# Rows of u and v side by side: one 8 KB gather per expert slot, in a ring of eight pairs

## What is computed

```
def peer(h, w_query, sub_keys, u, v):        # u, v: (16384, 1024) per layer
    q = h @ w_query                          # 8 heads, two halves of 128
    s = q . sub_keys                         # 2 x 128 scores per head
    top_s, top_i = top_k(s, 16)              # per half
    best_s, best_pos = top_k(all 256 sums, 16)
    expert = ...                             # 16 numbers per token and head
    gate = softmax(best_s)
    act = gelu(h . u[expert])                # one dot product of 1024 per expert
    y += (gate * act) * v[expert]            # summed over 8 heads x 16 experts
```

## Time and profile before

| | |
|---|---|
| median of 3 runs | 1996.8 us (1992.76 to 1998.14) |
| profiled execution | 1994.14 us |
| its span, first to last instruction | 1992.4 us |
| mean granted TensorE clock | 0.815 |
| busy: PE, DVE, ACT, POOL | 1480.2, 1171.5, 279.1, 1025.0 us |
| DMA bytes | 669.91 MB, mean 336 GB/s |

### The profile page before, as it was taken

One profiled execution on the slowest core, in us unless ns is written; L12 is line 12 of the kernel. 1 busy time (PEld: TensorE's weight loads), 2 busy tenths in 40 slices (PEclk: granted clock), 3 DMA queues, 4 the chain that ended last, 5 costly groups with the idle time before them and its releaser, 6 DMA issues.

```text
span 1992.4 us, 18966 instructions
## 1 busy us (share of the span) xinstructions
PE 1480.2 (74%) x6422; PEld 589.7 (30%) x6422; DVE 1171.5 (59%) x2700; ACT 279.1 (14%) x539; POOL 1025.0 (51%) x1099
## 2 busy tenths in 40 slices
PE   6978999784577656767788886677797766666666
PEld 5736666464233210102223222022232210101100
DVE  3541000158777757687669636966776587776752
ACT  2141111211101101001212111012321110010000
POOL 2000000004777766677456655775566577677674
PEclk9988999877788765668996988689888975667678
DMA  9123346106999999999999999999999999999998
GB/s 332 58 80 135 130 163 256 75 22 207 383 409 409 409 409 410 396 410 409 409 406 372 410 409 393 410 409 409 404 337 409 410 409 409 406 410 408 391 404 326
DMA packets 189385, 669.91 MB, mean 336 GB/s; under 512 B 19806, under 2 KB 20960, under 8 KB 188016
## 3 DMA queue, kind: packets, MB, share of 16 engines
q0 software_dynamic: 152064, 553.72, 70.6%
q1 hardware_dynamic: 37232, 115.09, 15.2%
HBM read 667.68 MB, written 1.05 MB: 336 GB/s over the span
## 4 chain that ended last, share of the span: by engine, by line
DMA 32%; PE 15%; DVE 13%; POOL 12%; issue 6%; DVEq 2%; ACT 1%; POOLq 0%; ACTq 0%
DMA big<-in_peer_v,expert 25%; POOL big L506 12%; DVE big L569 8%; DMA big<-in_peer_u,expert 7%; PE ps L552 5%; PE ps L692 3%; PE ps L535 2%; DVEq L446 2%; PE ps L334 2%; PE ps L786 1%; PE ps L788 1%; PE ps L1658 0%; DVE residual L599 0%; PE ps L696 0%; DVE half_v L452 0%
## 5 line engine op out<-in xcount | busy, mean ns | idle before, releaser
L552 PE MATMUL ps<-big,diag 128*32 128x512 f32 (+1 forms) x2112 | 712.7, 794 | 434.5 <-DMA big<-in_peer_v,expert 399.9
L569 DVE CUSTOM_DVE_ANT_0 big<-big,ps 128x1024 f32<-128x1024 f32 x528 | 625.8, 1218 | 345.5 <-DMA big<-in_peer_u,expert 241.5
L506 POOL DMA_INDIRECT big<-in_peer_u,expert x528 | 502.1, 951 | 301.0 <-issue 131.1
L506 POOL DMA_INDIRECT big<-in_peer_v,expert x528 | 506.3, 959 | 257.2 <-PE ps L552 143.0
L552 PEld LDWEIGHTS ps<-big,diag 128*32 128x32 f32 (+1 forms) x2112 | 83.7, 120 | 968.1 <-DMA big<-in_peer_v,expert 851.6
L692 PE MATMUL ps<-big 128*128 128x512 f32 x384 | 199.0, 642 | 0.0
L1586 POOL MEMSET big<- 128x128 f32 x3 | 0.5, 203 | 374.1 <-POOLq L1450 374.1
L230 DVE RECIPROCAL stats<-stats 128x1 f32<-128x1 f32 (+1 forms) x17 | 2.7, 161 | 252.0 <-ACT stats L224 251.6
L1506 PE MATMUL ps<-ua,big 128*128 128x256 f32 x512 | 116.3, 382 | 0.0
L1517 PE MATMUL ps<-big,sc 128*128 128x512 f32 x256 | 114.4, 592 | 0.0
L1506 PEld LDWEIGHTS ps<-ua,big 128*128 128x128 f32 x512 | 98.3, 192 | 25.4 <-issue 13.2
(11 more groups left out here) (293 smaller groups left out, 1185.6 us busy)
## 6 DMA issues: line engine op xcount, KB each, us to landing
big<-in_mlp_w SPq DMA_DIRECT2D x16, 2048.0 KB, 7.8
big<-in_w_kv SPq DMA_DIRECT2D x32, 512.0 KB, 6.8
big<-in_peer_wq SPq DMA_DIRECT2D x32, 512.0 KB, 6.8
big<-in_w_in SPq DMA_DIRECT2D x5, 2048.0 KB, 17.7
big<-in_peer_u,expert POOLq DMA_INDIRECT x528, 9.5
big<-in_peer_v,expert POOLq DMA_INDIRECT x528, 9.7
big<-in_peer_wq SPq DMA_DIRECT2D x1, 8192.0 KB, 27.1
big<-in_w_q SPq DMA_DIRECT2D x16, 512.0 KB, 7.3
```

Source lines behind the costliest of these rows:

```text
L506: nc.gpsimd.indirect_dma_start(out=ring[n % len(ring)], out_offset=None, in_=rows[name], in_offset=bass.IndirectOffsetOnAxis(ap=expert[:, ...
L552: last = nc.tensor.matmul(acc[r:r + tokens, :], placed(u, tokens)[:, k, :], ring_v[n % len(ring_v)][:, BANK * half:BANK * (half + 1)], sta ...
L569: nc.vector.tensor_tensor_reduce(out=slot, in0=slot, in1=rows_x, scale=1.0, scalar=0.0, op0=ALU.mult, op1=ALU.add, accum_out=dots[:, u % 2 ...
```

## The change

In memory the rows of `u` and `v` of the same expert are put side by side ahead of the launch, as one table with 8 KB rows. One gather per slot then brings 128 rows of 8 KB into one of eight pair buffers (seven in `big`, which grows by 528 columns, and one in `normed` and later at the end of `big`); the buffer is free only when the slot's `v` products are done. The `v` work no longer runs 22 slots behind: ScalarE computes, slot by slot, gelu of the mask times the dot, then times the gate, into a 128 x 32 weight tile, and TensorE follows with that slot's products. Softmax division moves to VectorE (`gates_of`). The routing of units 1 to 4 and of the first units of layer 1 is dealt out anew, `unit_rows` is issued ahead of the last slot of the group before, the attention starts four steps earlier, and its score stage takes eight steps where it took six (`STEPS`).

```diff
-RING_U = 7
-RING_V = 6
+RING = 8
...
-        V_BEHIND = TOPK + 6
+        SLOT_MOVES = 7 * TOPK
...
+        EARLY = {(0, 0): (1, (2,)), (0, 1): (1, (3,)), (0, 2): (2, (0,)), (0, 3): (2, (1,)), (1, 0): (2, (2,)),
...
         def peer_gpsimd(pool):
-            for i in range(SLOTS + V_BEHIND):
-                if i < SLOTS:
-                    if i % TOPK == 0:
-                        pool.wait_ge(S("experts_ready"), i // TOPK + 1)
-                    gather("u", i)
-                if i == V_BEHIND:
-                    pool.wait_ge(S("ffn0_scores_done"), META_UNIT + 1)
-                if i >= V_BEHIND:
-                    gather("v", i - V_BEHIND)
+            rows = peer_uv.rearrange("l e d -> (l e) d")
+            for n in range(SLOTS):
+                if n % TOPK == 0:
+                    pool.wait_ge(S("experts_ready"), n // TOPK + 1)
+                if n == 6:
+                    pool.wait_ge(S("ffn0_scores_done"), META_UNIT + 1)
+                if n == SLOT_MOVES + RING - 1:
+                    pool.wait_ge(S("ffn0_q_done"), 4 * PH)
+                if n >= RING:
+                    slots_done(pool, "v_used", n - RING + 1)
+                nc.gpsimd.indirect_dma_start(
+                    out=pair_row(n), out_offset=None, in_=rows,
...
         def slot_value(pe, n):
-                pe.wait_ge(S("weights_ready"), u + 1)
-            pe.wait_ge(S(f"v{n % len(ring_v)}_loaded{UNITS[u][0]}"), loads_of(n, len(ring_v)))
+            slots_done(pe, "weights_ready", n + 1)
...
+        def gates_of(dve, u):
+            dve.wait_ge(S("gates_exp"), u + 1)
+            v.reciprocal(gate_sum[:, at:at + 1], gate_sum[:, at:at + 1])
+            dve.drain()
+            v.tensor_scalar(gate[:, at, :], gate[:, at, :], gate_sum[:, at:at + 1], None, ALU.mult)\
+                .then_inc(S("gates_ready"), 1)
+        def slot_weight(act, n):
+            same, to = (sel16 if tokens == META else sel32)[:], placed[:, n % RING, 0:tokens]
+            slots_done(act, "dots_done", n + 1)
+            if n >= RING:
+                slots_done(act, "v_used", n - RING + 1)
+            a.activation(to, same, ACT.Gelu, scale=dots[:, u % 2, k:k + 1])
+            if k == 0:
+                act.wait_ge(S("gates_ready"), u + 1)
+            act.drain()
+            a.activation(to, to, ACT.Copy, scale=gate[:, u % DEEP, k:k + 1]).then_inc(S(f"weights_ready{UNITS[u][0]}"), 1)
...
         def peer_scalar(act):
+            gates_exp(act, 0)
+            for s in range(units):
                 for j in range(4):
+                    x = 4 * s + j
+                    for q in range(4):
+                        slot_weight(act, 4 * x + q)
+                        if q == 1:
+                            late_queries_act(act, x)
+                            for t in range(NT):
+                                attend_act(act, t, x - ATTEND[t])
+                        if (j, q) == (3, 0) and s + 1 < units:
+                            gates_exp(act, s + 1)
...
         def peer_tensor(pe):
+                        if (j, q) == (3, 3) and s + 1 < units and opens_group(s + 1):
+                            unit_rows(pe, s + 1)
+                        slot_value(pe, 4 * x + q)
...
-        ATTEND = (42, 74)
+        ATTEND = (38, 70)
+        STEPS = ((0,), (1,), (2, 3), (4,), (5,), (6, 7), (8, 9), (10, 11))
```

More of the change, by code:

```diff
@@ L605, in peer_vector @@
             v = nc.vector
+            for stage in range(4):
+                route(dve, 0, stage)
+            for stage in range(2):
+                route(dve, 1, stage)
+            gates_of(dve, 0)
             units = len(UNITS)
-            for u in range(2):
-                for stage in range(4):
-                    route(dve, u, stage)
             for s in range(units):
                 for j in range(4):
+                    ahead = j == 0 and s > 0 and opens_group(s)
+                    if ahead:
+                        routes_at(dve, s, j)
                     dots_of(dve, s, range(4 * j, 4 * j + 4))
-                    if j == 0 and s >= 1:
-                        weights_of(dve, s - 1)
-                    if j == 1 and s >= 2 and closes_group(s - 2):
-                        add_group(dve, s - 2)
-                    routes_at(dve, s, j)
+                    if j == 1 and s >= 1 and closes_group(s - 1):
+                        add_group(dve, s - 1)
+                    if not ahead:
+                        routes_at(dve, s, j)
                     if (s, j) == (PH - 2, 3):
@@ L789, in pv @@
                 last.then_inc(S("a_pv"), 1)
-            if 0 <= loop < 6 and q % 2 == 0:
-                n = 2 * loop + q // 2
+            for n in steps_at(loop)[q // 2:q // 2 + 1] if q % 2 == 0 else ():
                 if n < KD:
@@ L798, in attend_pe @@
                     pv(n - 4)
-            for k in {5: range(0, 4), 6: range(4, 8)}.get(loop, ())[q:q + 1]:
+            late = loop - AFTER
+            for k in {5: range(0, 4), 6: range(4, 8)}.get(late, ())[q:q + 1]:
                 if k == 0:
@@ L803, in attend_pe @@
                 product(pe, t, C_O, k, att_y[:, k, :], 6)
-            if loop == 8 and q == 0:
+            if late == 8 and q == 0:
                 pe.wait_ge(S("f_normed"), ONE["f_normed"] * t + 1)
@@ L824, in attend_pe @@
                 last.then_inc(S("f_q_t"), 1)
-            if loop in (12, 15) and q == 0:
-                half = (loop - 12) // 3
+            if late in (12, 15) and q == 0:
+                half = (late - 12) // 3
                 pe.wait_ge(S("f_q_out"), ONE["f_q_out"] * t + half + 1)
@@ L945, in y_out @@
                     .then_inc(S("a_y_out"), 1)
[L947 to L955 removed]
+            late = loop - AFTER
+            for n in steps_at(loop):
+                if n < KD:
+                    sigmoids(n)
+                if 2 <= n < KD + 2:
+                    weights_out(n - 2)
+                if n >= 4:
+                    y_out(n - 4)
+            if late == 7:
                 act.wait_ge(S("f_h3"), ONE["f_h3"] * t + 1)
@@ L958, in attend_act @@
                 act_root_mean(act, P, t, "f")
-            if loop == 8:
+            if late == 8:
                 act.wait_ge(S("f_t"), ONE["f_t"] * t + 1)
@@ L964, in attend_act @@
                         .then_inc(S("f_t_out"), 1)
-            if loop in (10, 13):
-                half = (loop - 10) // 3
+            if late in (10, 13):
+                half = (late - 10) // 3
                 product_done(act, t, C_P + KD * half)
@@ L970, in attend_act @@
                 a.activation(raw, bank(6 - 2 * half, 2), ACT.Copy).then_inc(S("f_rows"), 1)
-            if loop in (11, 14):
-                half = (loop - 11) // 3
+            if late in (11, 14):
+                half = (late - 11) // 3
                 act.wait_ge(S("f_q_t"), ONE["f_q_t"] * t + half + 1)
@@ L976, in attend_act @@
                     .then_inc(S("f_q_out"), 1)
-            if loop in (12, 15):
-                half = (loop - 12) // 3
+            if late in (12, 15):
+                half = (late - 12) // 3
                 act.wait_ge(S("f_scores"), ONE["f_scores"] * t + half + 1)
@@ L1044, in attend_dve @@
                     .then_inc(S("a_q_out"), 1)
-            if 0 <= loop < 4:
+            late = loop - AFTER
+            if any(n < KD for n in steps_at(loop)):
                 if loop == 0:
@@ L1051, in attend_dve @@
                     dve.drain()
-                for n in (2 * loop, 2 * loop + 1):
+                for n in steps_at(loop):
                     dve.wait_ge(S("a_keep"), ONE["a_keep"] * t + n + 1)
```

164 lines of the change are left out of this document (74 added, 90 removed).

## The result

| | before | changed |
|---|---|---|
| median, runs side by side | 1997.5 us (1992.8 to 2001.9, 4 runs) | 1978.2 us (1977.7 to 1978.6, 4 runs) |
| ratio | | 0.990, interval 0.988 to 0.993 |
| profiled execution, its span | 1994.14, 1992.4 us | 1978.63, 1976.9 us |
| granted TensorE clock | 0.815 | 0.809 |

The changed kernel is 19 us faster. I had predicted 1930 us, 67 less than before. The direction is right, the size is less than a third of it, and the time lies just above the range.

The account below looks back on a forecast made before the run. The prediction took the DMA engines' ceiling of 409 GB/s to bound the kernel. Its terms summed as 1994.1 - 45 - 14 - 5 - 1 = 1929 us, stated as 1930, with a range of 1903 to 1977.

Parts of the forecast that it names:

- The bound: Whole gather stage: the DMA engines stand at a ceiling of 409 GB/s; only 41 of 1528 us are lost.
- The sign that I had set: Whole gather stage: a mean rate below 409 GB/s would show the prediction wrong.
- Term 1: All gathers: 8 KB rows instead of 4 KB raise the rate from 409 to 423 GB/s, saving 45 us.
- Rival A: Gathers: 8 KB rows are cut, or memory rather than packets is the limit; nothing saved there, 1975 us; chance 0.12.
- Term 2: Start of the gather stage: eight pairs go out ahead of any product, saving 14 of 18 lost us.
- Term 3: Middle of the stage: losses at group changes mostly go, the attention's 12 us stay; saving 5 us.
- The slack of 8.6 us: Loop of one pair buffer: at most 11.2 us of its 19.8 are used, leaving 8.6 for lateness.
- Term 4: End of the stage: losses of the last 26 us shrink by some 3, last row's work adds 2; saving 1 us.
- The milder B: Attention: slot weights wait behind ScalarE's copies and stop gathers, 20 to 40 us lost, 1950 to 1970 us; chance 0.12.
- the rival's own counterargument: Attention copies: most earlier waiting was ScalarE being early; now its slots pace it, and TensorE's part stands ahead.
- B outright: Attention: waits in ScalarE's queue beyond the slack stop the gathers for 83 us, 2013 us; chance 0.11.
- C: Start and group changes go better still, attention dips vanish, rows run at 425 GB/s: 1908 us; chance 0.08.

Follow-up runs that it names:

- e13: Changed kernel with two gathers of 4 KB rows per slot instead of one of 8 KB: 2012.5 us, against 1999.5 for the kernel before on the same chip.
- e7: Changed kernel with TensorE's attention products behind the step's second slot and ScalarE's last copies behind the third slot's weight: 1957.1 us, 0.981 of the kernel before.
- e3: Changed kernel with the attention's score stage in six steps of two head pairs instead of eight steps: 1993.3 us.
- e5: The changed kernel again, unedited, against the kernel before on the same chip: 1977.2 us, ratio 0.991 (0.987 to 0.994).
- e10: The changed kernel unaltered, on a chip where the kernel before takes about 2127 us: 1981.5 us (1979.2 to 1982.1).
- e1: Changed kernel with two gathers of 4 KB rows per slot, on a slow chip: 2144.6 us, against 2126.6 for the kernel before there, ratio 1.008.
- e4: Changed kernel with seven pair buffers instead of eight: 1987.3 us (1985.8 to 1990.7).

## Why the prediction was wrong

**The bound** was named rightly: the DMA engines stand at their ceiling outside the dips, before and after. The sign that I had set, a mean of the stage below 409 GB/s, came about: 402.

**Term 1, -45 us, came to -39.** Without dips the gathers run at 421, the value computed from the rates of 2 and 4 KB rows, and not at the 423 that I took between it and the load of `peer_wq`: 553.7 MB take 1353.8 - 1315.2 = 38.6 us less. e13 gives 35 for the same thing by a direct swap, on a kernel whose dips cover some of it. Rival A is excluded. By the rule of the Trainium skill ("DMA: Bandwidth & Descriptors", "Why small descriptors are slow") it would have been an estimated 20 us; both measurements are nearer to twice that. The prediction called the fixed part of 9.2 ns "more than twice as large" as the rule's. It is just under twice: 4 beats beside 128 that take 151 ns are 4.7 ns.

**Term 2, -14 us, came to -15.** The start of the stage moves 400 GB/s instead of 279, and three of the 18 lost us remain. The seventh gather waited for an earlier product (L369), which the prediction had not counted, but six pairs in the queue cover that. The step on which it rested also held: the ninth gather goes out at 477.94, where I had set buffer 0 free at about 477.

```profile
471.41 0.94 POOL L522 DMA_INDIRECT big<-in_peer_uv,expert  x1 [5.72 <-PE ps L369]
472.65 0.94 POOL L522 DMA_INDIRECT normed<-in_peer_uv,expert  x1 [0.30 <-issue]
477.94 0.94 POOL L522 DMA_INDIRECT big<-in_peer_uv,expert  x1 [4.35 <-PE ps L556]
```

**Term 3, -5 us, is the step that failed.** Its first half held: the waits at a change of group fell to 13.0 us, and outside attention, start and end only some 3 us of transfer are lost. Its second half, "there I expect the 12 lost us again", said of the attention stretches, measured 50. Three things in it were wrong.
- I argued from VectorE's busy share. The slot's weight had moved to ScalarE, and ScalarE's place in a score step was never added up. The sum can be read off the timeline: four weights 4 x 0.64, sigmoids with their loads 2 x 1.28 + 0.7, copies 0.8, in one step in four an exponential with its loads 3.0, and the wait for TensorE 2.75. That is 6.6 us of work, 9.6 with the exponential, and 9.4 and 12.4 with the wait, against a pace of 10.0 per four slots.
- I priced gelu and gate product at 0.22 us each, by an ACTIVATE on a 128 x 16 tile; they took 0.32. The Trainium skill ("ScalarE: Activation LUTs", "What ACT_TABLE_LOAD costs") adds about 93 ns for a per-partition operand, which is what these two have as their scale: by its formula 0.31 us, and the trace agrees.
- The slack of 8.6 us was set against single delays one at a time. (One sum beside it was off as well: 5.3 + 3.4 is 8.7 and does not quite fit in 8.6.) In a score step they are in series, and each crosses between TensorE and ScalarE, which both work in program order. e7 shows it: the same instructions, with the same loads, in another order give back 20 us. e3 fits it in the other direction: heavier steps cost 12.

**Term 4, -1 us, came to about +6.** The last pair lands at 1967.7, 15.7 us behind its issue, and the end comes 9.2 us later instead of 6.3: dot, weight and products now stand in series behind the last bytes. And the rate falls before that. The moved bytes from 1930 to 1970 us, one value per us:

```profile
GB/s 418 426 434 418 393 418 442 426 401 418 426 434 418 418 410 451 426 393 426 426 434 418 418 401 459 426 393 426 401 369 156 139 57 25 25 25 33 0 0 0
```

Most DMA engines are done at 1960, and for the last four us what moves is one engine's share of the rate, about 25 GB/s (421/16 = 26). A slot is done only when the slowest is.

**The sum.** Of the 50 us between forecast and result, about 6 are term 1, about 38 the attention, some 7 the end, and the start gives 1 back. On chip B the swap tells the same: all but the row length was forecast at -20 and costs 13.

**The rivals.** The milder B, at 0.12, named the mechanism that decides: ScalarE's attention work stands ahead of the slots' weights, and buffers come free only behind it. But it named the copies at L910 and L1000, whose counterparts had the longest waits of ScalarE in the earlier trace rows. They came to 19.5 and 6.4 us instead of 60.3 and 74.4, as the rival's own counterargument had it. The place is the score stage, whose 31.5 us of waits stood in the trace of the kernel before but not in the earlier trace rows. B outright didn't come, C was excluded by the dips.

## What to carry to other kernels

When per-item work moves to another engine, add up that engine's whole program for one period of the ring, table loads and in-line waits included, and compare it with the ring's pace; a busy share of 37% (553 of 1512 us) hides steps that take it longer than the pace. Two engines that run in program order and hand work to each other within a step put everything behind them on one chain, and splitting the step so that neither stands waiting ahead of an item was worth as much as removing the table loads. When DMA is the bound, a longer row was worth what the rates at shorter rows say.

## What the runs showed of the hardware that I had not expected

- **With 4 KB gathers some chips are slow.** On A and C the kernel before takes 2127 us and the one with two 4 KB gathers per slot 2145 and 2143, on B 1995 to 2000 and 2012; with 8 KB rows the changed kernel takes 1981 on C and 1977 on B. So the change is worth 0.991 on B (e5) and 0.932 (0.929 to 0.935, e10) on C. The rows themselves are hardly slower: the 152064 packets of the gathers take 67.8% of the 16 engines' 2142.5 us in e1, that is 1453, and 69.8% of 2011.1 us in e13, 1404, so they account for 49 of the 131 us between the two spans. TensorE is slower too in e1: before the 256 matmuls of the layer-1 scores (L866), which wait for nothing but the start of each of their four groups, it stands still 34 times for 24.9 us, and 4 times for 2.4 us in e13. The cause isn't shown, nor whether the chip or the placement of the tables in its memory decides.
- **The 16 DMA engines drift apart.** At the end of the changed kernel, with eight pairs queued, the last bytes land some 7 us after most engines are done; in the kernel before, with less queued, the rate falls to nothing within 2 us of its last full microsecond. The row length is not the reason: e13, with 4 KB rows in the same ring, ends with 25, 25 and 29 GB/s in three microseconds one after the other as well. e4, with seven buffers, has two of them (25 and 33), which would fit the depth of the queue. e1, whose engines are not full, has none.
- **The table load shows as 1.28 us** in every place, with the next ACTIVATE about 0.01 us behind it (1040.37 + 1.28, then 1041.66). The Trainium skill ("ScalarE: Activation LUTs", "What ACT_TABLE_LOAD costs") gives 2.66 us for a switch, load and drain together, and no drain of that size is seen here, ahead of the load or behind it.
